# Gate and up projections with features on the partitions: 128-column weight pieces stationary, 256 tokens moving

## The chip, the cores and the metric

The kernel runs on one core of a Trainium2 chip. The metric is the device time of one execution in microseconds (us); three runs of the kernel before gave 2680.31, 2683.87 and 2687.0 us.

## What is computed

Two transformer-like blocks in float32 over one sequence of 256 tokens of width 2048. The change touches two places. The first is the gated feed-forward part that closes block one (hidden width 5632), the second is the Fourier mixer of block two (hidden width 4096, groups of 256 features):

```python
h2 = _modulate(_rms(x, norm2_w[i]), shift2, scale2).astype(x.dtype)
ffn = (jax.nn.silu(h2 @ w_ffn_gate[i]) * (h2 @ w_ffn_up[i])) @ w_ffn_down[i]
...
def fourier_mixer(h, w_in, w_out):
    b, l, _ = h.shape
    u, gate = jnp.split(h @ w_in, 2, axis=-1)
    ug = u.reshape(b, l, C_GROUPS, C_GROUP_DIM).astype(jnp.float32)
    f = jnp.fft.fft2(ug, axes=(1, 3), norm="ortho").real.astype(h.dtype)
    y = f.reshape(b, l, C_WIDTH) * jax.nn.silu(gate)
    return y @ w_out
```

Both have one form: a gate projection, an up projection, a product of silu(gate) with the up result (in the Fourier mixer with its two-dimensional transform), and a down projection. Everything before, between and after them (state space mixer, attention, norms, modulation) is left as it is.

## The kernel before

**Precision.** A float32 product is made of three matmuls on numbers that are split in a high and a low part (`float32r`): high by high, high by low, low by high. Activations stand turned, with the 2048 inputs on the partitions: `hh` and `hl` are [128, 16, 256] (16 k-tiles, 256 tokens). Weights are streamed from memory in units of 256 rows by 512 columns (512 KB): the SyncE queue loads a unit in one of 8 raw slots (`load`, L179), ScalarE writes its high part (`high`, L185), VectorE its low part (`low`, L191), TensorE uses it (`multiply`, L198). There are 4 slots for the split units: ScalarE may write unit u only when TensorE has finished unit u - 4 (semaphore `s_mm`).

**A unit on TensorE (`multiply`).** For each of 2 k-tiles and 2 token tiles it issues three matmuls (L206, L207, L208): a 128 x 128 piece of `hh` or `hl` is stationary and 512 weight columns move. That is 12 matmuls with 512 columns. The result has tokens on the partitions: PSUM banks 0 and 1 take the gate, banks 2 and 3 the up result.

**The steps.** Class `Hidden` (L1418) describes either part. A step c handles 512 hidden features and its order is written out by hand for each engine: units j = 0 to 7 are the gate, 8 to 15 the up projection, 16 to 23 are the down projection of the step before (the first step has 16 units, and 8 down units stand behind the last). The feed-forward part has 11 steps, the Fourier mixer 8, so the gate and up projections are 16 x 19 = 304 units. TensorE walks through them in `hidden_pe` (L1761), ScalarE in `hidden_act` (L1512), VectorE in `hidden_dve` (L1596), SyncE in `hidden_sp` (L1436).

**Between up and down.** ScalarE makes silu of the gate at its j = 11 (L1496). In the feed-forward part VectorE multiplies it with the up result at its j = 19 (L1564) into `hid` [128 tokens, 2, 512]. In the Fourier mixer VectorE copies the up result to `ub` (L1559), TensorE does the first transform after unit 19 (`hidden_dft1_pe`), ScalarE stores it at its j = 23 (`hidden_store_act`), TensorE does the second after unit 3 of the next step (`hidden_dft2_pe`), and VectorE combines and multiplies at its j = 7 (`hidden_product_dve`, L1566).

**The turn.** The down projection needs the hidden features on the partitions, so TensorE turns `hid` in two groups of four 128 x 128 transposes into PSUM bank 6 (`hidden_turn_pe`, L1700, the transposes are L1713). ScalarE makes the high part `hidh` from that bank (L1483), VectorE the low part `hidl` (L1489). The second group waits until VectorE has read the first (semaphore `H.l`). `TURN_AT` gives the places: in the feed-forward part TensorE turns after units 1 and 9 and the other two work at their j = 6 and 14; in the Fourier mixer after units 9 and 12, and at 13 and 16. At the end of each part (`hidden_end_pe`, and for the feed-forward part the head of the context stage, L1973) the turn of the last step stands right ahead of its down units.

**Down projection.** `hidden_down_pe` (L1746) has `hidh` and `hidl` stationary and 512 weight columns moving, and the change leaves that as it is.

**Other work on TensorE in these steps** are modulation rounds (L266) and sums (L354), one or two in a step. A piece of code elsewhere, `ctx_mult` (L1909), already multiplies the other way round: 128 weight columns stationary, 256 tokens of `ch_h` and `ch_l` moving (L1924, L1925, L1926).

## Time and profile before

| | before |
|---|---|
| median of 3 runs | 2683.87 us (2680.31 to 2687.0) |
| profiled execution | 2680.69 us |
| its span, first to last instruction | 2678.9 us |
| TensorE matmul busy | 2496.6 us, 93% |
| TensorE weight loads busy | 1935.3 us, 72% |
| VectorE busy | 1637.4 us, 61% |
| ScalarE busy | 1035.1 us, 39% |
| memory traffic, mean over the span | 220 GB/s |
| feed-forward steps | about 603 to 1404 us of the span |
| Fourier mixer steps | about 2027 to 2679 us of the span |

A busy TensorE says that matmuls are in flight, not how fast they follow each other: a matmul with 512 columns is recorded with about 0.39 us, and the next one begins 0.23 us after its start. What a matmul takes from the engine is the distance between starts, so these are read from the order of instructions in time. The profiled execution lasted 1.8 us longer than its span.

### The profile page before, as it was taken

Reading aid. Unit: us, or ns where it says so; the run is one execution under the profiler, and the core shown is the slowest. Engines: PE = TensorE matmul, PEld = TensorE weight load, DVE = VectorE, ACT = ScalarE, POOL = GpSimd, SP = SyncE. Lnnn points to the kernel's source line nnn. Section 1 sums busy time; section 2 is a strip of 40 time slices with the busy share of each in tenths; the row PEclk is TensorE's granted clock in tenths of the full one; section 3 lists DMA queues with packets and bytes.
Section 4 is the critical chain, followed back from the end, with each engine's and each line's share of the span. In section 5 each row is a group of like instructions: output and inputs, shape, how many; then the busy total and the mean of one; then the engine's idle time right before and its main releaser. Section 6 shows DMA issues by size and latency. Waiting matters only on the chain.

```text
span 2678.9 us, 30714 instructions
## 1 busy us (share of the span) xinstructions
PE 2496.6 (93%) x11822; PEld 1935.3 (72%) x11822; DVE 1637.4 (61%) x1954; ACT 1035.1 (39%) x1370; POOL 214.9 (8%) x193
## 2 busy tenths in 40 slices
PE   5899787989999999999999999999897999999995
PEld 1588665558777777777777887777675788888884
DVE  8544544356777887775667565443466485765556
ACT  2343654224333333333343454444332333334331
POOL 0127810002000000000011000000002000000000
PEclk8799898999999999999999999998897999999997
DMA  9744458986999999997453753333364476675451
GB/s 392 271 150 134 125 216 302 342 334 223 344 338 350 360 338 333 338 336 271 152 173 108 236 154 112 97 97 118 113 194 141 162 249 193 217 239 178 154 171 40
DMA packets 278034, 588.99 MB, mean 220 GB/s; under 512 B 20608, under 2 KB 29824, under 8 KB 276608
## 3 DMA queue, kind: packets, MB, share of 16 engines
q1 hardware_dynamic: 277888, 587.02, 63.6%
q8 instruction: 94, 1.54, 0.2%
q14 instruction: 52, 0.43, 0.0%
HBM read 584.85 MB, written 2.10 MB: 219 GB/s over the span
## 4 chain that ended last, share of the span: by engine, by line
PE 84%; DVE 5%; DMA 3%; POOL 3%; ACT 2%; issue 2%; SPq 0%; DVEq 0%; ACTq 0%; POOLq 0%
PE psum L206 24%; PE psum L208 23%; PE psum L207 23%; PE psum L266 3%; DMA start_slots<-in_w_ada 2%; PE psum L2340 1%; POOL pool_scan_tmp L765 1%; PE psum L1725 1%; DVE wlo L195 1%; PE psum L2315 1%; PE psum L2314 1%; POOL xacc L765 1%; PE psum L1713 1%; DMA x<-in_x 1%; PE psum L681 1%
## 5 line engine op out<-in xcount | busy, mean ns | idle before, releaser
L195 DVE TENSOR_TENSOR wlo<-raw,whi 128x1024 fp32r<-128x1024 f32 (+2 forms) x728 | 880.1, 1227 | 685.1 <-ACT whi L189 672.3
L189 ACT CAST whi<-raw 128x1024 fp32r<-128x1024 f32 (+2 forms) x728 | 738.2, 1025 | 976.2 <-PE psum L208 886.0
L206 PE MATMUL psum<-whi,hh 128*128 128x512 f32 (+1 forms) x2080 | 844.2, 406 | 35.4 <-DVE wlo L195 34.8
L208 PE MATMUL psum<-whi,hl 128*128 128x512 f32 (+1 forms) x2080 | 819.4, 394 | 0.0
L207 PE MATMUL psum<-wlo,hh 128*128 128x512 f32 (+1 forms) x2080 | 817.3, 393 | 0.0
L206 PEld LDWEIGHTS psum<-whi,hh 128*128 128x128 f32 x2080 | 395.9, 190 | 160.7 <-issue 66.8
L208 PEld LDWEIGHTS psum<-whi,hl 128*128 128x128 f32 x2080 | 395.4, 190 | 89.1
L207 PEld LDWEIGHTS psum<-wlo,hh 128*128 128x128 f32 x2080 | 396.5, 191 | 82.7 <-issue 2.9
L206 PE MATMUL psum<-whi,hidh 128*128 128x512 f32 x608 | 247.6, 407 | 8.0 <-DVE wlo L195 6.0
L207 PE MATMUL psum<-wlo,hidh 128*128 128x512 f32 x608 | 243.3, 400 | 0.0
L208 PE MATMUL psum<-whi,hidl 128*128 128x512 f32 x608 | 243.0, 400 | 0.0
L343 DVE SCALAR_TENSOR_TENSOR powers<-araw,cond,powers 128x512 f32<-128x512 f32 x300 | 225.2, 751 | 14.4 <-DVE powers L343 0.5
L402 POOL TENSOR_TENSOR rstd<-ms,mhalf 128x2 f32<-128x2 f32 x7 | 9.9, 1409 | 2027.8 <-DVE ms L387 744.4
L206 PEld LDWEIGHTS psum<-whi,hidh 128*128 128x128 f32 x608 | 116.1, 191 | 43.9 <-issue 14.0
L208 PEld LDWEIGHTS psum<-whi,hidl 128*128 128x128 f32 x608 | 116.0, 191 | 28.3
L207 PEld LDWEIGHTS psum<-wlo,hidh 128*128 128x128 f32 x608 | 116.2, 191 | 27.8 <-issue 0.7
L1588 DVE TENSOR_TENSOR xacc<-xacc,psum 128x1024 f32<-128x1024 f32 x68 | 82.9, 1219 | 29.9 <-PE psum L208 29.9
L266 PE MATMUL psum<-start_slots,cond_windows 128*32 128x512 f32 x256 | 47.5, 845 | 35.4 <-DMA start_slots<-in_w_ada 35.4
L266 PEld LDWEIGHTS psum<-start_slots,cond_windows 128*32 128x32 f32 x256 | 7.5, 133 | 69.0 <-issue 68.9
L414 PE MATMUL psum<-ident,xacc 128*128 128x128 f32 x128 | 25.2, 343 | 33.5 <-DVE xacc L396 21.3
L439 POOL TENSOR_TENSOR hl<-h,hh 128x512 fp32r<-128x512 f32 x32 | 46.6, 1465 | 118.6 <-ACT hh L434 118.6
L414 PEld LDWEIGHTS psum<-ident,xacc 128*128 128x128 f32 x128 | 19.4, 176 | 39.7 <-DVE xacc L396 21.7
(345 smaller groups left out, 2091.5 us busy)
## 6 DMA issues: line engine op xcount, KB each, us to landing
araw<-in_ada_w SPq DMA_DIRECT2D x128, 512.0 KB, 6.5
raw<-in_w_in_fourier SPq DMA_DIRECT2D x128, 512.0 KB, 4.1
raw<-in_w_ffn_gate SPq DMA_DIRECT2D x88, 512.0 KB, 9.6
raw<-in_w_ffn_up SPq DMA_DIRECT2D x88, 512.0 KB, 7.6
raw<-in_w_ffn_down SPq DMA_DIRECT2D x88, 512.0 KB, 9.7
raw<-in_w_in_attn SPq DMA_DIRECT2D x88, 512.0 KB, 4.3
araw<-in_w_ada SPq DMA_DIRECT2D x80, 512.0 KB, 6.2
start_slots<-in_w_ada SPq DMA_DIRECT2D x64, 512.0 KB, 7.7
```

The lines of the kernel that those rows point to most:

```text
L189: nc.scalar.copy(whi[:, u % SPLITS, 0:kn, 0:w], raw[:, u % RING, 0:kn, 0:w]).then_inc(s_hi, 1)
L195: nc.vector.tensor_tensor(wlo[:, u % SPLITS, 0:kn, 0:w], raw[:, u % RING, 0:kn, 0:w], whi[:, u % SPLITS, 0:kn, 0:w].bitcast(F32), ALU.subt ...
L206: nc.tensor.matmul(o, ah[:, kt + k, a], h, start=(kt + k == first_kt), stop=False)
L207: nc.tensor.matmul(o, ah[:, kt + k, a], lw, start=False, stop=False)
L208: ins = nc.tensor.matmul(o, al[:, kt + k, a], h, start=False, stop=(kt + k == last_kt))
L266: ins = nc.tensor.matmul(psum[32 * g:32 * g + 32, SET_BANKS[st][0]], condz[:, vectors - 1, kt, 3 - pi:35 - pi], slot(2 * r + e)[0][:, half ...
L343: ins = nc.vector.scalar_tensor_tensor(out=dst, in0=w, scalar=s, in1=dst, op0=ALU.mult, op1=ALU.add)
L414: ins = nc.tensor.transpose(psum[:, banks[r % 2], j * S + t * P:j * S + t * P + P], xn[:, t, kt * P:(kt + 1) * P], ident[:])
L439: nc.gpsimd.tensor_tensor(ol[:, 2 * r:2 * r + 2], h32[:, r % 2], oh[:, 2 * r:2 * r + 2].bitcast(F32), ALU.subtract).then_inc(s_hl, 1)
L681: ins = nc.tensor.matmul(psum[:, 4 + b, 32 * g:32 * g + 32], W[:, ri, 16 * b + g].rearrange("p i c -> p (i c)"), cpad[:, ri, 16 * b + g], ...
L765: ch(isa.tensor_tensor(o, a, b, op))
L1588: nc.vector.tensor_tensor(o, o, psum[:, BANK[n]:BANK[n] + 2], ALU.add).then_inc(H.dv, 1)
```

## The change

Gate and up units are multiplied by a new function, `multiply_turned`. For each of 2 k-tiles and 4 pieces of 128 weight columns it issues three matmuls with the weight piece stationary and the 256 tokens of `hh` or `hl` moving: 24 matmuls with 256 columns. The result has 128 features on the partitions and 256 tokens on the free axis, two pieces in each PSUM bank; banks, silu and product keep their shapes, and `hid` is already what the down projection wants. `hidden_turn_pe` and its semaphore `H.t` go. ScalarE and VectorE split `hid` directly from SBUF, at j = 6 and 9 (feed-forward) or 11 and 13 (Fourier). The two transforms keep the number and the shapes of their matmuls and work on the turned arrangement: the first now sums over features, the second over tokens. The down projection waits for the low part of each half at its first and second unit.

```diff
@@ -206,6 +206,18 @@
                 nc.tensor.matmul(o, ah[:, kt + k, a], h, start=(kt + k == first_kt), stop=False)
                 nc.tensor.matmul(o, ah[:, kt + k, a], lw, start=False, stop=False)
                 ins = nc.tensor.matmul(o, al[:, kt + k, a], h, start=False, stop=(kt + k == last_kt))
+        ins.then_inc(s_mm, 1)
+
+    def multiply_turned(pe, u, kt, bank):
+
+        pe.wait_ge(s_lo, u + 1)
+        for k in range(2):
+            for f in range(4):
+                o = psum[:, bank + f // 2, f % 2 * S:(f % 2 + 1) * S]
+                h, lw = (w[:, u % SPLITS, k, f * P:(f + 1) * P] for w in (whi, wlo))
+                nc.tensor.matmul(o, h, hh[:, kt + k], start=(kt + k == 0 and f % 2 == 0), stop=False)
+                nc.tensor.matmul(o, lw, hh[:, kt + k], start=False, stop=False)
+                ins = nc.tensor.matmul(o, h, hl[:, kt + k], start=False, stop=(kt + k == KT - 1 and f % 2 == 1))
         ins.then_inc(s_mm, 1)
 
     def lat(b0):
@@ -1419,8 +1431,8 @@
         def __init__(self, name, u0, wg, wu, wd, gcol, ucol, steps, fourier):
             self.u0, self.wg, self.wu, self.wd, self.gcol, self.ucol = u0, wg, wu, wd, gcol, ucol
             self.steps, self.fourier = steps, fourier
-            self.sg, self.a, self.t, self.h, self.l, self.dv, self.ub, self.f1, self.v, self.f2 = (
-                sem(name + n) for n in ("_silu", "_product", "_turned", "_high", "_low", "_added", "_up", "_dft1",
+            self.sg, self.a, self.h, self.l, self.dv, self.ub, self.f1, self.v, self.f2 = (
+                sem(name + n) for n in ("_silu", "_product", "_high", "_low", "_added", "_up", "_dft1",
                                         "_dft1_stored", "_dft2"))
 
         def unit(self, c, j):
@@ -1475,18 +1487,18 @@
             src = w_rows(H.wd, 4 * (c - 1) + 2 * (jj % 2), 2)[:, :, (jj // 2) * CW:(jj // 2 + 1) * CW]
             load(sp, H.u0 + 24 * c - 8 + jj, src)
 
-    def hidden_turn_act(act, H, c, r):
-
-        act.wait_ge(H.t, c * 2 + (r - 1))
+    def hidden_high_act(act, H, c, r):
+
+        act.wait_ge(H.a, c)
         if r == 0:
             act.wait_ge(s_mm, H.used(c, -1))
-        nc.scalar.copy(hidh[:, 2 * r:2 * r + 2], psum[:, 6].rearrange("p (a b) -> p a b", a=2)).then_inc(H.h, 1)
-
-    def hidden_turn_dve(dve, H, c, r):
+        nc.scalar.copy(hidh[:, 2 * r:2 * r + 2], hid4[:, 2 * r:2 * r + 2]).then_inc(H.h, 1)
+
+    def hidden_low_dve(dve, H, c, r):
         dve.wait_ge(H.h, c * 2 + (r - 1))
         if r == 0:
             dve.wait_ge(s_mm, H.used(c, -1))
-        nc.vector.tensor_tensor(hidl[:, 2 * r:2 * r + 2], psum[:, 6].rearrange("p (a b) -> p a b", a=2),
+        nc.vector.tensor_tensor(hidl[:, 2 * r:2 * r + 2], hid4[:, 2 * r:2 * r + 2],
                                 hidh[:, 2 * r:2 * r + 2].bitcast(F32), ALU.subtract).then_inc(H.l, 1)
 
     def hidden_silu_act(act, H, c):
@@ -1500,14 +1512,15 @@
         act.wait_ge(H.f1, c + 1)
         if c >= 1:
             act.wait_ge(H.f2, c)
-        o = dfts[:].rearrange("p (g h) k -> p h g k", g=2)
-        v = psum[:, 2:4].rearrange("p h (g k) -> p h g k", g=2)
+        o = dfts[:].rearrange("p (g t) k -> p t g k", g=2)
+        v = psum[:, 2:4].rearrange("p t (g k) -> p t g k", g=2)
         nc.scalar.copy(o[:, :, :, 0:129], v[:, :, :, 0:129])
         nc.scalar.copy(o[:, :, :, 257:384], v[:, :, :, 129:256])
         nc.scalar.copy(o[:, :, :, 129:256], v[:, :, :, 127:0:-1])
         nc.scalar.mul(o[:, :, :, 385:512], v[:, :, :, 255:128:-1], -1.0).then_inc(H.v, 1)
 
-    TURN_AT = {False: ((1, 6), (9, 14)), True: ((9, 13), (12, 16))}
+    PARTS_AT = {False: (6, 9), True: (11, 13)}
+    hid4 = hid[:].rearrange("p t (f s) -> p (t f) s", f=2)
 
     def hidden_act(act, H, c):
         first = isinstance(c, int) and c == 0
@@ -1517,8 +1530,8 @@
         for j in range(4 if first else 0, 16 if first else 24):
             if not first:
                 for r in range(2):
-                    if j == TURN_AT[H.fourier][r][1]:
-                        hidden_turn_act(act, H, c, r)
+                    if j == PARTS_AT[H.fourier][r]:
+                        hidden_high_act(act, H, c, r)
             if j == 11:
                 hidden_silu_act(act, H, c)
             if not H.fourier and c == 9:
@@ -1544,7 +1557,7 @@
     def hidden_end_act(act, H):
         c = H.steps
         for r in range(2):
-            hidden_turn_act(act, H, c, r)
+            hidden_high_act(act, H, c, r)
         for jj in range(8):
             high(act, H.u0 + 24 * c - 8 + jj)
 
@@ -1560,7 +1573,8 @@
         else:
             dve.wait_ge(H.sg, c + 1)
             if later:
-                dve.wait_ge(H.t, c * 2)
+                dve.wait_ge(H.h, c * 2)
+                dve.wait_ge(H.l, c * 2)
             nc.vector.tensor_tensor(hid[:], sgb[:], psum[:, 2:4], ALU.mult).then_inc(H.a, 1)
 
     def hidden_product_dve(dve, H, c):
@@ -1568,10 +1582,11 @@
         dve.wait_ge(H.f2, c + 1)
         dve.wait_ge(H.sg, c + 1)
         if not isinstance(c, int) or c >= 1:
-            dve.wait_ge(H.t, c * 2)
-        o = ub[:].rearrange("p t (g k) -> p t g k", g=2)
-        v = psum[:, 2:4].rearrange("p t (g k) -> p t g k", g=2)
-        even, odd = v[:, :, :, 1:128], hid[:].rearrange("p t (g k) -> p t g k", g=2)[:, :, :, 129:256]
+            dve.wait_ge(H.h, c * 2)
+            dve.wait_ge(H.l, c * 2)
+        o = ub[:].rearrange("p g (h k) -> p g h k", h=2)
+        v = psum[:, 2:4].rearrange("p g (h k) -> p g h k", h=2)
+        even, odd = v[:, :, :, 1:128], hid[:].rearrange("p g (h k) -> p g h k", h=2)[:, :, :, 129:256]
         ch = chd[0]
         ch(nc.vector.tensor_copy(odd, v[:, :, :, 129:256]))
         ch.wait()
@@ -1604,8 +1619,8 @@
         for j in range(4 if first else 0, n):
             if not first:
                 for r in range(2):
-                    if j == TURN_AT[H.fourier][r][1]:
-                        hidden_turn_dve(dve, H, c, r)
+                    if j == PARTS_AT[H.fourier][r]:
+                        hidden_low_dve(dve, H, c, r)
                 if second and j == 3 and not H.fourier:
                     hidden_up_dve(dve, H, 0)
                 if not second and j in (1, 3):
@@ -1654,7 +1669,7 @@
             hidden_add_dve(dve, H, c - 1, n)
         hidden_product_dve(dve, H, c - 1)
         for r in range(2):
-            hidden_turn_dve(dve, H, c, r)
+            hidden_low_dve(dve, H, c, r)
         for jj in range(8):
             low(dve, H.u0 + 24 * c - 8 + jj)
             if jj in (5, 7):
@@ -1697,34 +1712,17 @@
                 nc.vector.scalar_tensor_tensor(out=x[:, t, cs], in0=x[:, t, cs], scalar=rstd[:, t], in1=lnb[:, cs],
                                                op0=ALU.mult, op1=ALU.add).then_inc(s_post, 1)
 
-    def hidden_turn_pe(pe, H, c, r):
-
-        if r == 0:
-            pe.wait_ge(H.a, c * 1)
-            if c >= 2:
-                pe.wait_ge(s_mod, (16 + 2 * (c > 2) + 2 * (c > 4)) if H.fourier else min(2 * c - 2, 16))
-            if not isinstance(c, int) or c >= 2:
-                pe.wait_ge(H.l, c * 2 - 2)
-        else:
-            pe.wait_ge(H.l, c * 2 - 1)
-        for j in range(2):
-            for t in range(TT):
-                k = 2 * r + j
-                ins = nc.tensor.transpose(psum[:, 6, j * S + t * P:j * S + t * P + P], hid[:, t, k * P:(k + 1) * P],
-                                          ident[:])
-        ins.then_inc(H.t, 1)
-
     def hidden_dft1_pe(pe, H, c):
 
         pe.wait_ge(H.ub, c + 1)
         if c == 0:
             pe.wait_ge(s_dft, 48)
-        for half in range(2):
+        for t in range(TT):
             for g in range(2):
-                for t in range(TT):
-                    ins = nc.tensor.matmul(psum[:, 2 + half, g * S:(g + 1) * S],
-                                           ub[:, t, g * S + half * P:g * S + half * P + P], dft[:, t],
-                                           start=(t == 0), stop=(t == TT - 1))
+                for half in range(2):
+                    ins = nc.tensor.matmul(psum[:, 2 + t, g * S:(g + 1) * S],
+                                           ub[:, g, half * S + t * P:half * S + t * P + P], dft[:, half],
+                                           start=(half == 0), stop=(half == 1))
         ins.then_inc(H.f1, 1)
 
     def hidden_dft2_pe(pe, H, c):
@@ -1733,21 +1731,22 @@
         if c == 0:
             pe.wait_ge(s_zero, 3)
         for g in range(2):
-            for t in range(TT):
-                o = psum[:, 2 + t, g * S:(g + 1) * S]
-                for half in range(2):
-                    nc.tensor.matmul(o[:, 0:129], dfts[:, 2 * g + half, t * P:t * P + P], dft[:, half, 0:129],
-                                     start=(half == 0), stop=(half == 1))
-                for half in range(2):
-                    ins = nc.tensor.matmul(o[:, 129:256], dfts[:, 2 * g + half, S + t * P:S + t * P + P], dft2[:, half, 1:128],
-                                           start=(half == 0), stop=(half == 1))
+            for half in range(2):
+                o = psum[:, 2 + g, half * S:(half + 1) * S]
+                for t in range(TT):
+                    nc.tensor.matmul(o[:, 0:129], dfts[:, 2 * g + t, half * P:half * P + P], dft[:, t, 0:129],
+                                     start=(t == 0), stop=(t == TT - 1))
+                for t in range(TT):
+                    ins = nc.tensor.matmul(o[:, 129:256], dfts[:, 2 * g + t, S + half * P:S + half * P + P], dft2[:, t, 1:128],
+                                           start=(t == 0), stop=(t == TT - 1))
         ins.then_inc(H.f2, 1)
 
     def hidden_down_pe(pe, H, c, jj, unit):
 
         n = jj // 2
+        if jj < 2:
+            pe.wait_ge(H.l, c * 2 - 1 + jj)
         if jj == 0:
-            pe.wait_ge(H.l, c * 2)
             if isinstance(c, int) and c == H.steps:
                 pe.wait_ge(H.dv, 4 * c - 5)
             else:
@@ -1774,15 +1773,12 @@
             if j == 8 and not first:
                 pe.wait_ge(H.a, c * 1)
             if j < 16:
-                multiply(pe, tiles=lat(2 * (j // 8)), kt=2 * (j % 8), last_kt=KT - 1, **H.unit(c, j))
+                multiply_turned(pe, H.unit(c, j)["u"], 2 * (j % 8), 2 * (j // 8))
                 if first and j < 4:
                     turn_pe(pe, k, xn, kn, j + 4, j + 5)
             else:
                 hidden_down_pe(pe, H, c, j - 16, H.unit(c, j))
             if not first:
-                for r in range(2):
-                    if j == TURN_AT[H.fourier][r][0]:
-                        hidden_turn_pe(pe, H, c, r)
                 if H.fourier and j == 3:
                     hidden_dft2_pe(pe, H, c - 1)
                 if H.fourier and j == 19:
@@ -1810,8 +1806,6 @@
         c = H.steps
         if H.fourier:
             hidden_dft2_pe(pe, H, c - 1)
-        for r in range(2):
-            hidden_turn_pe(pe, H, c, r)
         for jj in range(8):
             hidden_down_pe(pe, H, c, jj, {"u": H.u0 + 24 * c - 8 + jj})
 
@@ -1972,7 +1966,7 @@
         for n in (2, 3):
             hidden_add_dve(dve, ffn, c - 1, n)
         for r in range(2):
-            hidden_turn_dve(dve, ffn, c, r)
+            hidden_low_dve(dve, ffn, c, r)
         for k in range(-8, 3 * UPC):
             if k == -8:
                 dve.wait_ge(s_growc, 8)
```

## Rows read from the trace of the kernel before

**Rows 1.** The page of the profile: busy time of each engine.
```profile
PE 2496.6 (93%) x11822; PEld 1935.3 (72%) x11822; DVE 1637.4 (61%) x1954; ACT 1035.1 (39%) x1370; POOL 214.9 (8%) x193
```

**Rows 2.** By window: busy PE, PEld, DVE, ACT, POOL; granted clock, DMA share, GB/s.
```profile
764.00:838.00 74.00, 74.00 (x352) 57.03 (x344) 58.06 (x65) 27.21 (x28) 0.00 (x0) 1.00 0.93 341
...
2252.00:2326.00 74.00, 74.00 (x344) 61.24 (x343) 45.56 (x46) 28.63 (x32) 0.00 (x0) 1.00 0.59 196
```

**Rows 3.** TensorE in time (start, length in us): gate and up units, 34 starts apart.
```profile
2283.17 0.39 PE L208 MATMUL psum<-whi,hl 128*128 128x512 f32 x1
...
2290.95 0.39 PE L206 MATMUL psum<-whi,hidh 128*128 128x512 f32 x1
```

**Rows 4.** TensorE in time: 256 tokens moving over stationary weights, 28 starts apart.
```profile
1483.81 0.28 PE L1925 MATMUL psum<-ctxh,wlo 128*128 128x256 f32 x1
...
1487.16 0.28 PE L1926 MATMUL psum<-ctxl,whi 128*128 128x256 f32 x1
```

**Rows 5.** TensorE in time: the same stage with 512 weight columns moving, 24 starts apart.
```profile
1446.28 0.39 PE L206 MATMUL psum<-whi,ctxh 128*128 128x512 f32 x1
...
1451.91 0.39 PE L206 MATMUL psum<-whi,ctxh 128*128 128x512 f32 x1
```

**Rows 6.** TensorE in time: stationary activations, 320 weight columns moving, 95 starts apart.
```profile
1509.90 0.31 PE L206 MATMUL psum<-whi,hh 128*128 128x320 f32 x1
...
1523.83 0.31 PE L208 MATMUL psum<-whi,hl 128*128 128x320 f32 x1
```

**Rows 7.** TensorE in time: sixteen matmuls with one column each.
```profile
861.95 1.84 PE L354 MATMUL psum<-ones,powers 128*128 128x1 f32 x16
863.65 0.48 PE L206 MATMUL psum<-whi,hidh 128*128 128x512 f32 x1
```

**Rows 8.** Groups of weight loads by shape (busy us, mean ns).
```profile
L1924 PEld LDWEIGHTS psum<-ctxh,whi 128*128 128x128 f32 x16 | 3.0, 188 | 1.4 <-DVE wlo L195 1.4
```

**Rows 9.** The line of the transposes: count, lengths, first and last start.
```profile
L1713 PE MATMUL psum<-ident,hid x152: 270/272/476, 659.9 to 2629.9; 128*128 128x128 f32 x152
```

**Rows 10.** TensorE in time around one group of transposes.
```profile
807.50 0.39 PE L208 MATMUL psum<-whi,hl 128*128 128x512 f32 x1
807.74 0.60 PE L1713 MATMUL psum<-ident,hid 128*128 128x128 f32 x4
...
808.41 0.40 PE L207 MATMUL psum<-wlo,hh 128*128 128x512 f32 x1
```

**Rows 11.** All engines in time: the end of the feed-forward part.
```profile
1392.98 0.40 PE L208 MATMUL psum<-whi,hidl 128*128 128x512 f32 x1
...
1393.42 1.22 DVE L1588 TENSOR_TENSOR xacc<-xacc,psum 128x1024 f32<-128x1024 f32 x1 [4.40 <-PE psum L208]
1393.86 0.59 ACT L1483 CAST hidh<-psum 128x512 fp32r<-128x512 f32 x1 [10.57 <-PE psum L1713]
...
1397.61 3.50 DVE L195 TENSOR_TENSOR wlo<-raw,whi 128x1024 fp32r<-128x1024 f32 x3 [0.31 <-ACT whi L189]
1398.98 0.77 PE L206 MATMUL psum<-whi,hidh 128*128 128x512 f32 x1 [3.03 <-DVE wlo L195]
```

**Rows 12.** All engines in time: the end of the Fourier mixer.
```profile
2625.50 1.23 DVE L1582 TENSOR_TENSOR hid<-sgb,ub 128x1024 f32<-128x1024 f32 x1
...
2631.91 4.63 DVE L195 TENSOR_TENSOR wlo<-raw,whi 128x1024 fp32r<-128x1024 f32 x4 [0.26 <-ACT whi L189]
2633.28 0.77 PE L206 MATMUL psum<-whi,hidh 128*128 128x512 f32 x1 [2.97 <-DVE wlo L195]
```

**Rows 13.** Who waited for whom, 640 to 1400 us (total us, times, longest).
```profile
ACT whi L189 <- PE psum L208: 400.4, 213, 4.2
...
PE psum L206 <- DVE wlo L195: 3.0, 1, 3.0
```

**Rows 14.** In time: VectorE's low parts of units 8 and 9, TensorE starting unit 9.
```profile
819.27 2.47 DVE L195 TENSOR_TENSOR wlo<-raw,whi 128x1024 fp32r<-128x1024 f32 x2
...
828.63 0.39 PE L206 MATMUL psum<-whi,hh 128*128 128x512 f32 x1
```

## Prediction

> **What bounds the kernel now.** I read the page first: TensorE is busy for 93% of the span, no other engine for more than 61% [rows 1]. A share says little by itself, so the second view is busy time by window. In a feed-forward step and in a Fourier step TensorE is busy for the whole window at a granted clock of 1.00, its upper level of 2.4 GHz, while VectorE is busy for 58.1 of 74.0 us at most and ScalarE for 28.6 [rows 2]. In these steps whatever TensorE does more or less in its instruction stream is on the path that sets the end, to the nanosecond. The third view is TensorE's order in time, because the recorded length of a matmul (0.39 us with 512 columns) overlaps the next one; what counts is the distance between starts. Over 34 starts in gate and up units this is (2290.95 - 2283.17) / 34 = 0.2288 us; I take 0.229 [rows 3].
>
> **Part 1: two matmuls of 256 columns in place of one of 512.** A unit has 12 matmuls now and 24 afterwards; columns that move are the same in number (12 x 512 = 24 x 256). There are 304 such units, so 304 x 12 = 3648 times one distance of 0.229 us is replaced by two distances at 256 columns. The trace has nearly this operation: in the context stage pieces of `whi` and `wlo` are stationary and 256 tokens move. Over 28 starts, four unit borders among them, the distance is (1487.16 - 1483.81) / 28 = 0.1196 us [rows 4]. This is more than half of 0.229. But the same stage with the same activation tile and 512 moving columns is slower too: (1451.91 - 1446.28) / 24 = 0.2346 us [rows 5]. So part of the 0.1196 may belong to that tile and not to the column count. A second way to the number stays with `hh`: with 320 columns its distance is (1523.83 - 1509.90) / 95 = 0.1466 us [rows 6]; the line through 320 and 512 columns has a slope of (0.229 - 0.1466) / 192 = 0.429 ns a column and gives 0.1466 - 64 x 0.000429 = 0.1191 us at 256. In the changed unit the weights are stationary as in rows 4 and `hh` moves, which neither row has. I take 0.1194, between the two and nearer to the row with the same roles: 2 x 0.1194 - 0.229 = 0.0098 us, and 3648 x 0.0098 = +35.8 us. The ends: 0.1196 gives +37.2 us. For the lower end I take the ratio of the two 512-column distances as if it held at 256 as well, 0.1196 x 0.229 / 0.2346 = 0.1167, which gives 3648 x 0.0044 = +16.1 us.
>
> Is there a floor under these small matmuls? Sixteen matmuls with a single column take 863.65 - 861.95 = 1.70 us, 0.106 us each, and about 0.11 with the late first one behind them [rows 7]. So one stationary load with its matmul has room in 0.12 us, with little to spare. Each load is recorded with 188 ns [rows 8]; if loads did not overlap, a unit would take 24 x 0.188 = 4.5 us and the change would cost 500 us, but rows 4 show one every 0.1196 us.
>
> The Trainium skill ("TensorE: Matmul & The Clock Gate", section "Back-to-back issue gap") lists 262 cycles for 256 columns and 518 for 512 at the upper clock. By these figures two matmuls of 256 would cost 2.5 ns more than one of 512, and the part would come to 3648 x 0.0025 = +9 us. The trace disagrees on both sizes: 0.1196 us where the page's cycles are 0.109, 0.229 where they are 0.216. I use the rows.
>
> **Part 2: the transposes go.** There are 152, in 38 groups of four [rows 9]. From the last matmul ahead of a group to the second behind it are 808.41 - 807.50 = 0.91 us [rows 10]; without the group these are two distances, 0.458 us. A group costs 0.45 us (the recorded 0.60 us is length, not cost). 34 groups stand inside a full stream: 34 x 0.45 = -15.3 us.
>
> The other four are at the two ends, where TensorE waits. Feed-forward end: its last matmul starts at 1392.98 and the next down unit at 1398.98 [rows 11]. Without the turn ScalarE can begin when that matmul is done, at about 1393.4 in place of 1393.86, and makes both high halves in a row (0.59 us each), until 1394.5; the first high part of weights follows, until about 1395.5. VectorE has its addition from 1393.42 for 1.22 us, then two low halves, until 1395.9, and the low weights begin there in place of 1397.61. That is 1.7 us earlier, and TensorE with it. Fourier end: the product is ready at 2625.50 + 1.23 = 2626.73 [rows 12]. Two high halves take until 2627.9, high weights until 2628.8, and low weights begin at about 2628.9 in place of 2631.91: 3.0 us. Both ends: -4.7 us.
>
> **Part 3: what is moved.** The splitting of `hid` reads SBUF in place of PSUM, with the same number of elements; it is on ScalarE and VectorE. New waits: ScalarE waits for the product `H.a` at its j = 6 or 11, with the high parts of weights (and in the Fourier mixer silu) queued behind. The product was made on VectorE at j = 19 of the step before or at j = 7, long before. Product and low part wait for each other on VectorE in order, at no cost. TensorE waits for the low halves at j = 16 and 17, made at 6 to 13. The cover is how far the weights' parts run ahead: in 760 us ScalarE waited 213 times for TensorE to free a slot, and TensorE waited for VectorE once, at the end of the part [rows 13]. VectorE had the low part of unit 9 at 821.7, TensorE began this unit at 828.63, 6.9 us later [rows 14]. Moving 0.68 us of VectorE from j = 14 to 9 is nothing against that, and every unit gives VectorE 0.12 us more. If the cover were gone, 38 halves of 0.6 us would cost 23 us. The transforms have the same counts and shapes: 0. SyncE's queue is not touched, and memory at 341 GB/s with a share of 0.93 in rows 2 only gets more time.
>
> **The sum.** +35.8 - 15.3 - 4.7 = +15.8 us. Against the profiled execution of 2680.69 us that is 2696.5. This execution lies 3.2 us under the median 2683.87 of the three runs shown, so I state 2699.7 us, +0.6%.
>
> **The rivals.**
> A, the forecast: small matmuls cost as above. Chance 0.66.
> B, the cost stays with the tile: if the distance at 256 columns comes out at 0.1167, the change costs 16.1 - 20.0 = -4 us, 2680 us, no difference. It turns at (0.229 + 20.0 / 3648) / 2 = 0.1172 us: below that the change does not lose. For it speaks that `hh` as an operand gives 2.4% shorter distances than the context tile at 512 columns; against it that the line by `hh` itself gives 0.1191. Chance 0.18.
> C, time goes by columns alone, with nothing for each matmul: 2 x 0.1145 = 0.229, part 1 is 0, and only the gains stay: 2664 us. For it: nothing but the floor of rows 7, which lies under 0.1145. Against it: rows 4. The skill's figures in part 1 belong here, at +9 - 20 = -11 us. Chance 0.08.
> D, borders: with starts so close to the floor TensorE's sequencer has no lead, and each unit's wait on the low part shows. Priced by a quarter of a matmul distance at 512, 0.06 us, in 304 units: 18 us more, 2718 us. Against it: four borders in rows 4 cost nothing. Chance 0.08.
>
> **How the numbers follow.** About 0.3% (8 us) is what a measurement of this kernel can tell from no change. In A the change stays within it if the distance is below 0.1183 us, which I give 0.04 of A's 0.66. So slower has 0.62 + 0.08 = 0.70, same 0.04 + 0.18 = 0.22, faster 0.08. The range takes in B and its few us of spread between runs, 2677, and above A's upper end, 0.1196 (2701), half of D and the spread between runs: 2712. C and most of D are left out.
>
> **What the profile after would show.** Starts in gate and up units at 0.1194 us (2.87 us a unit, 2.75 now); no transposes; a step of the feed-forward part longer by 16 x 12 x 0.0098 - 0.9 = 1.0 us; the waits for low weights at the two ends shorter by 1.7 and 3.0 us; clock 1.00 inside the steps. Wrong would make it: a distance under 0.1172; TensorE waiting for VectorE or ScalarE inside a step; a unit's first start late; a clock below 1.00.

## The result, and the profile after

The changed kernel takes 2666.6 us (median of 5 runs, 2665.8 to 2669.8); the kernel before, timed beside it, 2680.3 (5 runs, 2678.1 to 2687.0). The ratio is 0.9945, with an interval of 0.993 to 0.996: 13.7 us faster, where 16 us slower was forecast, with a range of 2677 to 2712 us. The profiled execution took 2667.0 us, its span is 2665.2 (2678.9 before).

First the page of the profile after (busy time by engine), then two windows of 74 us, in the feed-forward part and in the Fourier mixer, in the columns of [rows 2].

```profile
PE 2481.1 (93%) x15318; PEld 2083.2 (78%) x15318; DVE 1637.1 (61%) x1954; ACT 1034.3 (39%) x1370; POOL 214.3 (8%) x193
```

```profile
764.00:838.00 74.00, 74.00 (x542) 65.45 (x542) 59.25 (x67) 27.20 (x27) 0.00 (x0) 1.00 0.96 347
2252.00:2326.00 74.00, 74.00 (x525) 69.19 (x524) 47.66 (x50) 28.67 (x31) 0.00 (x0) 1.00 0.64 216
```

Matmuls went from 11822 to 15318: 3648 more, less 152 transposes, as the change says. TensorE still fills the windows at a clock of 1.00, so what it is given there is still the path. The answer to [rows 3], the order of TensorE in time, has two faces. Two stretches of gate and up units, 48 starts each:

```profile
1027.08 0.28 PE L220 MATMUL psum<-hl,whi 128*128 128x256 f32 x1
...
1032.52 0.28 PE L220 MATMUL psum<-hl,whi 128*128 128x256 f32 x1
...
1100.02 0.28 PE L220 MATMUL psum<-hl,whi 128*128 128x256 f32 x1
...
1105.67 0.28 PE L220 MATMUL psum<-hl,whi 128*128 128x256 f32 x1
```

The first stretch has (1032.52 - 1027.08) / 48 = 0.1133 us a start, the second, one step later and with the same instructions, (1105.67 - 1100.02) / 48 = 0.1177. All long stretches of the trace lie at one of these two values, or within 0.0004 us of them, and none changes inside: what breaks a stretch (down units, other small matmuls) is where the level can change. Taken from the first start of a unit to its last, 116 of the 304 units are at the low level, and 188 at the high one or slowed at the head of a stretch. The mean inside the stretches, where the clock is 1.00, is 0.1157 us. Neither level is near the 0.1194 of the forecast.

A step of the feed-forward part shows it by the sum. The first gate matmul of three steps in a row:

```profile
1017.88 0.39 PE L218 MATMUL psum<-hh,whi 128*128 128x256 f32 x1
...
1090.49 0.39 PE L218 MATMUL psum<-hh,whi 128*128 128x256 f32 x1
...
1164.75 0.39 PE L218 MATMUL psum<-hh,whi 128*128 128x256 f32 x1
```

The low step lasts 72.61 us, the high one 74.26; before, a step lasted 73.9. By the terms of the forecast a step should change by 384 x 0.1133 - 192 x 0.229 - 0.9 = -1.4 or by 384 x 0.1177 - 192 x 0.229 - 0.9 = +0.3 us, and it does.

The end of the feed-forward part, all engines in time (the answer to [rows 11]):

```profile
1385.10 0.40 PE L208 MATMUL psum<-whi,hidl 128*128 128x512 f32 x1
1385.53 1.22 DVE L1603 TENSOR_TENSOR xacc<-xacc,psum 128x1024 f32<-128x1024 f32 x1 [4.41 <-PE psum L208]
1385.59 1.14 ACT L1495 CAST hidh<-hid 128x512 fp32r<-128x512 f32 x2 [10.20 <-PE psum L208]
1386.63 3.89 ACT L189 CAST whi<-raw 128x1024 fp32r<-128x1024 f32 x4
1386.67 1.28 DVE L1501 TENSOR_TENSOR hidl<-hid,hidh 128x512 fp32r<-128x512 f32 x2
1387.88 2.35 DVE L195 TENSOR_TENSOR wlo<-raw,whi 128x1024 fp32r<-128x1024 f32 x2
...
1389.24 0.76 PE L206 MATMUL psum<-whi,hidh 128*128 128x512 f32 x1 [3.75 <-DVE wlo L195]
```

The gap from 1385.10 to 1389.24 is 4.1 us, before it was 6.0 [rows 11]. And the end of the Fourier mixer (the answer to [rows 12]):

```profile
2611.38 0.61 PE L1740 MATMUL psum<-dft,dfts 128*128 128x127 f32 x4
...
2614.14 1.23 DVE L1597 TENSOR_TENSOR hid<-sgb,ub 128x1024 f32<-128x1024 f32 x1
2615.40 1.14 ACT L1495 CAST hidh<-hid 128x512 fp32r<-128x512 f32 x2 [15.20 <-DVE hid L1597]
...
2617.52 2.36 DVE L195 TENSOR_TENSOR wlo<-raw,whi 128x1024 fp32r<-128x1024 f32 x2 [0.17 <-ACT whi L189]
2618.89 0.77 PE L206 MATMUL psum<-whi,hidh 128*128 128x512 f32 x1 [6.90 <-DVE wlo L195]
```

From VectorE's start on the last product to the next down unit: 4.75 us, before 2633.28 - 2625.50 = 7.78 [rows 12], so 3.0 us less. Both ends gave what they were forecast to give.

### The profile page after: what moved, and what is told of

Read it like the earlier page. It is cut to its first block, busy times and chain, and to the rows that moved or that the text cites. A ratio compares the mean times of both kernels' runs of the same rounds, so it can differ in the third digit from the quotient of the medians.

```text
span 2665.2 us, 37725 instructions
## 1 busy us (share of the span) xinstructions
PE 2481.1 (93%) x15318; PEld 2083.2 (78%) x15318; DVE 1637.1 (61%) x1954; ACT 1034.3 (39%) x1370; POOL 214.3 (8%) x193
## 4 chain that ended last, share of the span: by engine, by line
PE 84%; DVE 5%; DMA 3%; POOL 3%; ACT 2%; issue 2%; SPq 0%; DVEq 0%; ACTq 0%; POOLq 0%
PE psum L206 13%; PE psum L208 13%; PE psum L207 13%; PE psum L218 11%; PE psum L219 11%; PE psum L220 11%; PE psum L278 3%; DMA start_slots<-in_w_ada 2%; PE psum L2334 1%; POOL pool_scan_tmp L777 1%; PE psum L1723 1%; DVE wlo L195 1%; PE psum L2309 1%; PE psum L693 1%; PE psum L2308 1%
## 5 line engine op out<-in xcount | busy, mean ns | idle before, releaser
L218 PE MATMUL psum<-hh,whi 128*128 128x256 f32 x2432 | 686.6, 282 | 4.4 <-DVE wlo L195 4.4
L219 PE MATMUL psum<-hh,wlo 128*128 128x256 f32 x2432 | 679.8, 280 | 0.0
L220 PE MATMUL psum<-hl,whi 128*128 128x256 f32 x2432 | 679.7, 279 | 0.0
L218 PEld LDWEIGHTS psum<-hh,whi 128*128 128x128 f32 x2432 | 460.0, 189 | 26.8 <-issue 25.9
L220 PEld LDWEIGHTS psum<-hl,whi 128*128 128x128 f32 x2432 | 463.0, 190 | 0.0
L219 PEld LDWEIGHTS psum<-hh,wlo 128*128 128x128 f32 x2432 | 459.2, 189 | 1.3 <-issue 1.0
L206 PE MATMUL psum<-whi,hh 128*128 128x512 f32 (+1 forms) x864 | 354.8, 411 | 29.4 <-DVE wlo L195 28.9
L208 PE MATMUL psum<-whi,hl 128*128 128x512 f32 (+1 forms) x864 | 340.8, 394 | 0.0
L207 PE MATMUL psum<-wlo,hh 128*128 128x512 f32 (+1 forms) x864 | 339.5, 393 | 0.0
L207 PEld LDWEIGHTS psum<-wlo,hh 128*128 128x128 f32 x864 | 166.2, 192 | 34.3 <-issue 1.9
## 6 DMA issues: line engine op xcount, KB each, us to landing
raw<-in_w_ffn_gate SPq DMA_DIRECT2D x88, 512.0 KB, 10.8
```

Source lines behind the costliest of these rows:

```text
L206: nc.tensor.matmul(o, ah[:, kt + k, a], h, start=(kt + k == first_kt), stop=False)
L207: nc.tensor.matmul(o, ah[:, kt + k, a], lw, start=False, stop=False)
L208: ins = nc.tensor.matmul(o, al[:, kt + k, a], h, start=False, stop=(kt + k == last_kt))
L218: nc.tensor.matmul(o, h, hh[:, kt + k], start=(kt + k == 0 and f % 2 == 0), stop=False)
L219: nc.tensor.matmul(o, lw, hh[:, kt + k], start=False, stop=False)
L220: ins = nc.tensor.matmul(o, h, hl[:, kt + k], start=False, stop=(kt + k == KT - 1 and f % 2 == 1))
```

## The experiments

All are the changed kernel with one edit (in one case two), unless it is said that they are the kernel before. "Units low" counts the gate and up units at 0.1133 us, out of 304; the changed kernel has 116. Each ratio is to the kernel before, timed beside the run. The first question: is the level of the 256-column distance chance, or the roles of the operands, or the order of accumulation? The second, when none of these fitted: is it where the tiles lie in SBUF?

**The changed kernel again**, unaltered.

> The changed kernel, unaltered, profiled a second time. Its first profile shows two steady distances between starts in gate and up units: 0.1133 us (first step and steps 1 to 6 of the feed-forward part, first step of the Fourier mixer) and 0.1177 us (from step 7 on, and the other Fourier steps). If the level is fixed by the place in the instruction stream, the same units show the same level again and the time is within 2 us of 2666.6. If it is a state that the engine falls into, the units at 0.1133 and 0.1177 are others this time; each unit moved from one level to the other moves the time by 24 x 0.0044 = 0.11 us, so anything between 2650 (all low) and 2682 (all high).

2665.7 us (2663.7 to 2670.9), ratio 0.995 [0.9933, 0.9967]. 114 units are low. They are the same ones but for six units, three in the last feed-forward step and three at the start of the second Fourier step. So the levels are, but for a few units, not drawn anew in each execution.

**The kernel before, its gate and up matmuls in halves.** The activations stay stationary and the transposes stay; only the 512 columns are cut in two.

```diff
+                for half in range(2):
+                    c = slice(half * S, (half + 1) * S)
+                    o = psum[:, bank + t, c]
+                    h, lw = whi[:, u % SPLITS, k, c], wlo[:, u % SPLITS, k, c]
...
-                multiply(pe, tiles=lat(2 * (j // 8)), kt=2 * (j % 8), last_kt=KT - 1, **H.unit(c, j))
+                multiply_halves(pe, H.unit(c, j)["u"], 2 * (j % 8), 2 * (j // 8))
```

> The kernel before (activations stationary, the turn kept) with one edit: in gate and up units each matmul of 512 weight columns is made as two of 256. It changes the size alone, not the roles. Theory 1 (a matmul costs by its columns, whatever is stationary): distances of 0.113 to 0.118 us, the time changes by 3648 x (2 x 0.1155 - 0.229) = +7 us, between -9 and +24. Theory 2 (with stationary activations the line through 320 and 512 columns holds, and the gain came from the exchange of roles): 0.1191 us, +34 us.

2704.0 us, ratio 1.0096 [1.0063, 1.0128]. TensorE in time:

```profile
1042.42 0.28 PE L220 MATMUL psum<-whi,hh 128*128 128x256 f32 x1
...
1048.07 0.28 PE L220 MATMUL psum<-whi,hh 128*128 128x256 f32 x1
...
1192.69 0.28 PE L220 MATMUL psum<-whi,hh 128*128 128x256 f32 x1
...
1198.13 0.28 PE L220 MATMUL psum<-whi,hh 128*128 128x256 f32 x1
```

5.65 / 48 = 0.1177 and 5.44 / 48 = 0.1133: the same two values with the roles exchanged. Nearly all stretches here are at the high one, and 3648 x (2 x 0.1177 - 0.229) = +23 us is what the run shows over the kernel before. So which operand is stationary does not set the two values, though it or the rest of the kernel changes their mix (14 units low); and part 1 alone does cost time, as the forecast said, at a smaller size: +23 us where +35.8 was forecast.

**The changed kernel without its part 1**: gate and up by 512 columns again, with no turn of the product behind them (the product is used unturned, so the numbers it computes are others).

```diff
-                multiply_turned(pe, H.unit(c, j)["u"], 2 * (j % 8), 2 * (j // 8))
+                multiply(pe, tiles=lat(2 * (j // 8)), kt=2 * (j % 8), last_kt=KT - 1, **H.unit(c, j))
```

> The changed kernel with the old multiplication in gate and up units (stationary activations, 512 columns), and still no turn: only the transposes are gone. What is computed is not the reference's, since the product is used unturned. By the prediction's part 2 this is the kernel before minus 34 x 0.45 - 4.7 = 20.0 us, 2660 us. If the transposes had been cheaper than thought or something takes their place, less than 15 us. Against the changed kernel at 2666.6 it should be 6 us faster, if small matmuls cost 0.1158 us on average.

2657.0 us, ratio 0.9921 [0.9895, 0.9946]: 21 us less than the kernel before by the ratio (14 to 28), 24 between the medians. Steps of the Fourier mixer went from 76.17 and 74.37 us, in turn, to 75.27 and 73.48, 0.90 less each, which is two groups of transposes at 0.45. Part 2 stands with its -20.0 us. The run also measures part 1 in place, since it differs from the changed kernel in nothing else: 2666.6 - 2657.0 = +9.6 us. In the two traces the time from the start of each gate or up matmul to the next start on TensorE, one wait left out of each, adds up to 847.2 and 856.8 us: +9.6 again.

**Six matmuls in a row into one PSUM place**: the loop over the four pieces outside, the one over k inside.

```diff
-        for k in range(2):
-            for f in range(4):
+        for f in range(4):
+            for k in range(2):
```

> The changed kernel with the two loops of a unit exchanged: the piece outside, the k-tile inside, so that 6 matmuls in a row (in place of 3) accumulate in the same 256 columns of PSUM, as nearer to the context stage, where the distance is 0.1196 us and all 48 matmuls go to one place. If accumulating in one place costs distance, it rises from 0.113 to 0.118 to about 0.1196: +7296 x 0.0038 = +28 us. If what matters there is the moving tile, no change: 2664 to 2669 us.

2666.0 us, ratio 0.9947 [0.9931, 0.9962], with the same 116 units low. The order of accumulation does nothing.

**32 bytes left empty** ahead of the tiles of the mixers. In the compiled program `whi` and `wlo` begin at a multiple of 128 bytes in each partition and so do the pieces of them that a matmul reads; `hh` and `hl` begin 64 bytes past one, `hidh`, `hidl` and the context tile 96 past one. (These places follow from the order and the sizes of the tiles in the kernel.) The edit takes these last three to a multiple of 128.

```diff
+    pad_hidden = sb(ctx, "pad_hidden", [P, 8])
     m = ExitStack()
```

> The changed kernel with 32 bytes a partition of unused padding ahead of the tiles of the later stages. `hh` and `hl` stay where they are; `hidh`, `hidl`, the context tiles and the others behind them move from addresses that are 32 over a multiple of 64 to multiples of 64. Theory 1 (an operand that begins off a multiple of 64 bytes costs TensorE distance): down units, whose matmuls with 512 columns stand 0.2342 us apart, come to the 0.229 us of the units with `hh`, 608 x 3 = 1824 matmuls x 0.0053 = -9.7 us; the context stage's 256 columns come from 0.1196 to 0.113 to 0.118; the time is about 2656. Gate and up units keep their two levels. Theory 2 (the tile's distance has another cause): no distance changes, 2664 to 2669.

2661.3 us, ratio 0.9939 [0.9917, 0.9962]. The down units, which had (1014.68 - 1006.25) / 36 = 0.2342 us a start in the changed kernel, here have 0.2325:

```profile
1006.90 0.40 PE L207 MATMUL psum<-whi,hidh 128*128 128x512 f32 x1
...
1015.27 0.40 PE L207 MATMUL psum<-whi,hidh 128*128 128x512 f32 x1
```

Neither theory holds: the distance changed, but not to 0.229, and the context stage's 256 columns read 0.1184 to 0.1190 us, not 0.113 to 0.118. Of the gate and up units, whose own tiles did not move, 148 are low in place of 116. The time is less, but the interval overlaps that of the changed kernel; what the run gave is the idea.

**`hh` and `hl` moved by 192 bytes**, to a multiple of 128, with the tiles behind them at one too.

```diff
+    pad_hh = sb(ctx, "pad_hh", [P, 48])
     hh = sb(ctx, "hh", [P, KT, S], F32R)
...
+    pad_hidden = sb(ctx, "pad_hidden", [P, 24])
```

> As e5_pad32, and `hh` and `hl` too are moved, by 192 bytes, so that all matmul operands that are activations begin at multiples of 256 bytes. If finer alignment of the moving tile makes the two levels (0.1133 and 0.1177 us) in gate and up units, all of them come to the lower, 171 units x 24 x 0.0044 = -18 us against e5_pad32. If the levels are not a matter of address, the same units as before show 0.1177 us and the time is that of e5_pad32.

2692.3 us, ratio 1.0058 [1.0033, 1.0082]. TensorE in time: in the attention part 512 columns over `hh`, then a gate stretch of the Fourier mixer:

```profile
1502.21 0.39 PE L208 MATMUL psum<-whi,hh 128*128 128x512 f32 x1
...
1513.36 0.39 PE L208 MATMUL psum<-whi,hh 128*128 128x512 f32 x1
...
2204.41 0.29 PE L220 MATMUL psum<-hh,whi 128*128 128x256 f32 x1
...
2210.17 0.29 PE L220 MATMUL psum<-hh,whi 128*128 128x256 f32 x1
```

11.15 / 48 = 0.2323 where it was 0.229; 5.76 / 48 = 0.1200, and 0.1187 in other stretches. No stretch is left at 0.1133 or 0.1177, so the expectation that alignment brings all of them to the lower level is refuted. By the mean inside its stretches (0.1190) part 1 grows by 7296 x (0.1190 - 0.1157) = 24 us, and the median is 26 over the changed kernel, 31 over the run with 32 bytes left empty, from which it differs only in the place of `hh` and `hl` modulo 128 bytes. (The profiled execution, 2706.0, was the slowest of the seven; its steps are 20.7 us longer in sum.) 192 empty bytes ahead of `hh` cost 1% of the kernel.

**An extra, already met wait on TensorE** ahead of the second feed-forward step, to shift what follows in its instruction stream.

```diff
+        if not H.fourier and c == 1:
+            for _ in range(3):
+                pe.wait_ge(s_one, 16)
```

> The changed kernel with one more instruction in TensorE's stream, a wait that has long been met, ahead of step 1 of the feed-forward part. If the level belongs to a position in the instruction stream, it moves: some units of steps 1 to 6 at 0.1177 us, or some of the later ones at 0.1133. If it belongs to what goes on in the step (other engines, transfers), the pattern of the changed kernel stays: low in steps 1 to 6, high from 7 on.

2666.2 us, ratio 0.9953 [0.9936, 0.997]; the same 116 units are low. (One instruction came of the three.) A shift of the instruction stream by one instruction does not move the levels; larger ones were not tried.

**128 tokens a matmul**, twice as many of them again.

> The changed kernel with each matmul of gate and up units cut again, 128 tokens in place of 256, twice as many. If a load of the stationary operand takes about 0.106 us of the engine (sixteen matmuls with one column took 1.70 us), the distance stays near 0.107 us and a unit takes 48 x 0.107 = 5.1 us: +304 x 2.4 = +730 us, and 256 columns lie just above the floor. If there is no such floor, the distance halves to 0.057 us and the time stays within 20 us.

3758.7 us, one run. Two stretches of gate units:

```profile
700.10 0.41 PE L220 MATMUL psum<-hh,whi 128*128 128x128 f32 x1
...
705.22 0.41 PE L220 MATMUL psum<-hh,whi 128*128 128x128 f32 x1
...
1002.09 0.28 PE L220 MATMUL psum<-hh,whi 128*128 128x128 f32 x1
...
1007.45 0.28 PE L220 MATMUL psum<-hh,whi 128*128 128x128 f32 x1
```

The later one has 5.36 / 48 = 0.1117 us: with half the columns the distance hardly falls, from 0.1133. This is a floor, a little above the 0.106 of the one-column matmuls [rows 7]. The earlier one, 5.12 / 24 = 0.2133, lies where the granted clock was 0.50, the level of 1.2 GHz; twice as many matmuls at the floor cost 14592 x 0.1117 - 7296 x 0.1157 = 786 us. The rest of the 1092 us over the changed kernel, 306, is about what such stretches cost: the clock stood at 0.50 from 606 to 954 us, 1811 to 1907 and, but for 7 us, 2664 to 2910, together 683 us of which half, 341, is lost. The windows of 100 us:

```profile
700.00:800.00 100.00, 100.00 (x471) 100.00 (x470) 18.95 (x19) 11.35 (x11) 0.00 (x0) 0.50 0.23 76
...
1000.00:1100.00 100.00, 100.00 (x783) 91.56 (x782) 51.68 (x56) 23.83 (x24) 0.00 (x0) 1.00 0.66 221
```

The clock fell at 606 us, while TensorE waited for 8.0 us ahead of the first step. In the changed kernel it fell in the same wait, at 600 us, and was back at 1.00 at 610. Here it stayed down until 954 us, although TensorE was busy for 341 of the 342 us from 612 on. What kept it down is not shown. The fall at 1811 us came with no wait ahead of it.

**96 bytes left empty** ahead of the mixers' tiles, so that `hidh`, `hidl` and the context lie 64 past a multiple of 128, like `hh`.

```diff
+    pad_hidden = sb(ctx, "pad_hidden", [P, 24])
     m = ExitStack()
```

> The kernel after with 96 bytes a partition left empty ahead of the tiles that hold hidh, hidl and the context: their address goes from 96 to 64 bytes past a multiple of 128, where hh and hl lie. Theory (the address of the activation tile sets the distance of starts): the down units go from 0.234 to 0.229 us a matmul, 1824 x 0.0053 = 9.7 us less, the context's 256-column matmuls from 0.1196 to 0.113-0.118 us; time about 2655 us. Rival (the address of hidh has no effect beyond that of the padding by 32 bytes, or the gain there was chance): the down units stay at 0.2326-0.234 us and the time lies at 2661-2666 us.

2650.7 us (2649.8 to 2652.1), ratio 0.9886 [0.9873, 0.990], the fastest of all. A down stretch and a gate stretch at the place where the changed kernel was at the high level:

```profile
1010.98 0.39 PE L207 MATMUL psum<-whi,hidh 128*128 128x512 f32 x1
...
1019.22 0.39 PE L207 MATMUL psum<-whi,hidh 128*128 128x512 f32 x1
...
1118.03 0.28 PE L220 MATMUL psum<-hh,wlo 128*128 128x256 f32 x1
...
1123.47 0.28 PE L220 MATMUL psum<-hh,wlo 128*128 128x256 f32 x1
```

8.24 / 36 = 0.2289 and 5.44 / 48 = 0.1133. The down units give 1824 x 0.0053 = 9.7 us. Low units are 209 of 304, most of the new ones in the Fourier mixer, and the mean inside the stretches falls from 0.1157 to 0.1141, another 7296 x 0.0016 = 11.7 us. In the feed-forward part some units went to the low level and about as many to the high one; the gain is in the Fourier mixer. The sum, 21, is what the two parts lost in the profiled execution (20.5), and more than the 16 between the medians; the profiled executions differ also by 4.4 us in when the first step begins (608.56 and 612.98), ahead of the units that the edit speeds up.

The context stage, from which the forecast took its 0.1196, is the same code in all these runs. With its tile at 64 bytes from the weights it reads:

```profile
1473.09 0.28 PE L1921 MATMUL psum<-ctxl,whi 128*128 128x256 f32 x1
...
1475.81 0.28 PE L1921 MATMUL psum<-ctxl,whi 128*128 128x256 f32 x1
```

2.72 / 24 = 0.1133 us: the very operation of [rows 4] comes to a level of `hh` when its tile is moved.

**The kernel before with the same 96 bytes.**

> The kernel before with the same 96 bytes left empty. Theory: hidh and the context read as above, down units 0.229 us, 9.7 us less and a few us more in attention: about 2670 us, so that the distance between the two kernels with the padding stays near the 14 us that it has without. Rival (the kernel before gains nothing by it): 2680 us.

2671.7 us, ratio 0.9961 [0.9948, 0.9975]. Its down stretch:

```profile
1014.82 0.39 PE L207 MATMUL psum<-whi,hidh 128*128 128x512 f32 x1
...
1023.06 0.39 PE L207 MATMUL psum<-whi,hidh 128*128 128x512 f32 x1
```

And its context stage, the place of [rows 4]:

```profile
1482.23 0.28 PE L1927 MATMUL psum<-ctxl,whi 128*128 128x256 f32 x1
...
1485.41 0.28 PE L1927 MATMUL psum<-ctxl,whi 128*128 128x256 f32 x1
```

8.24 / 36 = 0.2289 again, and 3.18 / 27 = 0.1178, the other level of `hh`. The 8.4 us between the medians fit the 9.7 of the down units. With the padding in both, the change is worth 2671.7 - 2650.7 = 21 us in place of 14, since most of its gate and up units (209 of 304) are at 0.1133, where two of them cost 0.2266 and one of 512 costs 0.229.

**64 bytes left empty ahead of `whi`**: everything that a matmul reads moves by the same 64 bytes.

```diff
+    pad_w = sb(ctx, "pad_w", [P, 16])
     whi = sb(ctx, "whi", [P, SPLITS, 2, CW], F32R)
```

> The kernel after with 64 bytes left empty ahead of whi: whi, wlo, hh, hl, hidh and all later tiles move together by 64 bytes, so the distances between the addresses stay as they are, while hh is now at a multiple of 128. Theory that the distance between the two operands' addresses counts: nothing changes, gate and up 0.1133 and 0.1177 us, 2666 us. Rival, that the moving or stationary activation's own address counts: gate and up 0.1187-0.120 us as where hh alone was moved there, about 2690 us, and hidh (32 past a multiple of 128) at a distance not seen yet.

2667.4 us, ratio 0.9948 [0.9934, 0.9961]. The gate stretches are at 0.1133 and 0.1177 in the same places (the same 116 units low), the down units at 0.2342. The two stretches that answer those of the changed kernel:

```profile
1030.03 0.28 PE L221 MATMUL psum<-hl,whi 128*128 128x256 f32 x1
...
1035.47 0.28 PE L221 MATMUL psum<-hl,whi 128*128 128x256 f32 x1
...
1102.08 0.28 PE L221 MATMUL psum<-hl,whi 128*128 128x256 f32 x1
...
1107.73 0.28 PE L221 MATMUL psum<-hl,whi 128*128 128x256 f32 x1
```

`hh` is here at a multiple of 128, where it cost 0.119 to 0.120 above, and costs nothing. So it is not the address of a tile by itself that counts but its distance from tiles that moved with it. The weights are the ones among these that the same matmul reads, which is why the distance is taken here from the other operand; a third tile was not moved by itself to rule it out.

**32 bytes left empty ahead of `hh`**: `hh` 96 bytes past a multiple of 128, as the context tile is in the kernel before.

```diff
+    pad_hh = sb(ctx, "pad_hh", [P, 8])
     hh = sb(ctx, "hh", [P, KT, S], F32R)
```

> The kernel after with 32 bytes left empty ahead of hh: hh and hl lie 96 bytes past a multiple of 128, where the context tile lies in the kernel before, whose 256-column matmuls started 0.1196 us apart; later tiles lie at a multiple of 128. Theory (the 0.1196 us of the context belongs to its tile's address): gate and up 0.1196 us throughout, 3648 x 2 x (0.1196 - 0.1158) = 28 us over the kernel after, less about 3 us in the down units: about 2691 us. Rival (the 0.1196 us belongs to something else of the context's matmuls, its sources or its stage): 0.113-0.118 us, about 2663 us.

2697.4 us (2681.6 to 2700.3, 10 runs), ratio 1.0044 [1.0026, 1.0063]; the profiled execution, 2683.1, was among its fastest. A gate stretch, and 512 columns over `hh`:

```profile
1110.09 0.28 PE L219 MATMUL psum<-hh,whi 128*128 128x256 f32 x1
...
1115.77 0.28 PE L219 MATMUL psum<-hh,whi 128*128 128x256 f32 x1
...
1530.69 0.40 PE L207 MATMUL psum<-whi,hh 128*128 128x512 f32 x1
...
1541.89 0.40 PE L207 MATMUL psum<-whi,hh 128*128 128x512 f32 x1
```

5.68 / 48 = 0.1183 in every stretch, at one level, and 11.20 / 48 = 0.2333. This is not quite the 0.1196 of [rows 4], but it has left both values that `hh` had. By this distance the gate and up units cost 7296 x (0.1183 - 0.1157) = 19 us more than in the changed kernel, and the down units, now at 0.2325, 3 us less. The sum of 16 us is what the profiled execution shows (2683.1 against 2667.0); the median is 31 over. The spread of 19 us between runs is unexplained.

The distances, by how far the activation tile lies from the weights, modulo 128 bytes:

```text
bytes apart   256 columns                      512 columns
64            0.1133 or 0.1177 (hh)            0.229  (hh; hidh with 96 bytes left empty)
              0.1133, 0.1178 (context, with 96 bytes left empty)
0             0.1187 or 0.1200 (hh)            0.2323 (hh), 0.2325 (hidh)
              0.1184 to 0.1190 (context)
96            0.1183 (hh), 0.1196 (context)    0.2333 (hh), 0.2342 (hidh)
```

32 bytes apart was not tried.

## Why the prediction was wrong

**What bounds the kernel**: right. TensorE fills the steps at a clock of 1.00 before and after, and each step's length changed by what its distances say.

**Part 1** failed, and its failing step is the choice of 0.1194. The distance was taken from [rows 4], because there the weights are stationary as in the changed kernel. The halves in the kernel before showed that the roles do not make the difference: with the activations stationary the distances are 0.1133 and 0.1177 too. What rows 4 had of its own was the place of its tile, 96 bytes from the weights where `hh` is at 64: with that tile at 64, the same code reads 0.1133 in the changed kernel and 0.1178 in the kernel before. The prediction saw a sign of it, [rows 5] against [rows 3], 0.2346 against 0.229 at 512 columns with everything else alike, and put that in the lower end only, as a ratio. A difference between two rows with the same operation and the same shape is a second variable that has not been named; it should have been worked into the likeliest value. The measured mean of 0.1157 lies even under that lower end, 0.1167. The term is +9.6 us, by the changed kernel with and without part 1, where +35.8 was forecast; 3648 x (2 x 0.1157 - 0.229) gives +8.8.

The second way to the number, the line through 320 and 512 columns, stayed with `hh` and still gave 0.1191. Its other point was the fault: the 320-column matmuls start 0.1466 us apart with `hh` at each of the three distances tried. With `hh` 96 bytes from the weights, in the last of the experiments, where 256 and 512 columns had both become slower, they read

```profile
1516.36 0.31 PE L207 MATMUL psum<-whi,hh 128*128 128x320 f32 x1
...
1528.82 0.31 PE L208 MATMUL psum<-wlo,hh 128*128 128x320 f32 x1
```

(1528.82 - 1516.36) / 85 = 0.1466 us as in [rows 6]. So what slows the 512-column row does not slow this one, and a line through the two has no meaning at 256. That it met rows 4 was an accident, and two ways that agree were taken for a proof.

**The floor** in [rows 7] was read rightly: 0.1117 us at 128 columns, 0.106 at one. The Trainium skill ("TensorE: Matmul & The Clock Gate", section "LDWEIGHTS (loading the stationary operand)") gives the columns of the stationary piece by 1.2 as a load's time in ns, 107 for 128 columns. The runs agree with it as a floor (0.1117), not as a length of a load (0.188) [rows 8]. Cutting these matmuls from 256 to 128 columns therefore saved 0.0016 us a start at the most and cost a further start for each piece.

**Part 2** right: the run without part 1 gives -21 us (-28 to -14; -24 between the medians) against -20.0, the steps lost 0.90 us each for two groups, and the ends gained 6.0 - 4.1 = 1.9 and 3.0 us against 1.7 and 3.0.

**Part 3** right: nothing. TensorE waits three times inside the two parts (2.0, 1.3 and 4.4 us, for VectorE), and as long at the same places before; these are not of the change. The new waits for the low halves are met before TensorE comes to them.

**The sum** with the measured term: +9.6 - 20.0 = -10.4 us. The medians differ by 13.7 (the ratio's interval is 11 to 19 us). The two profiled executions, 13.7 apart as well, say where the rest is:

| stretch of the span | before | after | |
|---|---|---|---|
| start to the first gate matmul | 607.5 | 608.6 | +1.1 |
| from there to the first down unit after the last step | 791.5 | 780.7 | -10.8 |
| from there to the Fourier mixer | 633.1 | 630.0 | -3.1 |
| Fourier mixer, to the end | 646.8 | 645.9 | -0.9 |

The two parts that the change touches give -11.7. The -3.1 lies between them, where TensorE's code is the same, and stays open.

That the sum came out as a gain also hangs on the mix of the two levels, which nobody chose: with every unit at 0.1177 it would be 3648 x (2 x 0.1177 - 0.229) - 20.0 = +3 us, with every unit at 0.1133 it would be -29.

**The rivals.** D, a cost at the borders, is refuted: the 48 starts of each stretch above contain borders of units, at no cost. B gave the right cause, that the cost stays with the tile, at 2680 us, and C, columns alone, gave the nearest time, 2664 us, for a reason that is not true: two halves cost 0.2354 us at the high level, more than 0.229. Both had too little of the chance. The Trainium skill's figures ("TensorE: Matmul & The Clock Gate", section "Back-to-back issue gap"), 262 cycles for 256 columns and 518 for 512, gave +9 us for the part, and +9.6 was measured. But the distances were not its 0.109 and 0.216, and neither level has its ratio; the mean of the two comes near it by luck.

**What stays open**: what decides between 0.1133 and 0.1177 at the same address. It goes by place in the program, but for a few units. The order of accumulation and a shift by one instruction do not change it; with the roles exchanged both levels are there, but nearly all units are high. It is decided at the head of a stretch and holds to its end; and moving `hidh`, which the gate matmuls do not read, changes it, in the feed-forward part both ways. The units ahead of a gate stretch read `hidh`, so their rhythm may set it. That is argued, not shown. Nor is it shown why an address costs at all.

## What to carry to other kernels

Before a duration is carried from one row to another, compare two rows of the same operation and shape on the two tiles: if they differ (here 0.2346 and 0.229), the tile is a part of the price. In a kernel bound by a long stream of matmuls a few percent of the stream can lie in where the two operands stand to each other in SBUF: it is worth trying 32, 64 and 96 empty bytes ahead of a tile, since 96 ahead of the mixers' tiles gave 16 us in the changed kernel, more than the change itself, for one line, and 8 in the kernel before. And a padding tried for one stage must be read in all stages, since it moves every tile behind it: 192 bytes ahead of `hh`, with 96 more ahead of the mixers' tiles, cost 26 us.

## What the hardware showed that was not expected

- In these runs the distance between starts goes with the distance between the two operands' addresses modulo 128 bytes: at 512 columns 0.229 us at 64 bytes, 0.2323 and 0.2325 at 0, 0.2333 and 0.2342 at 96; and moving both operands by 64 bytes leaves it. At 320 columns it is 0.1466 us at all three. The Trainium skill ("SBUF — State Buffer", section "Who interferes with whom") gives TensorE two independent read ports, one for the moving operand and one for loads. Read as saying that the two operands cannot disturb each other, it does not fit these runs; it says nothing of addresses.
- At 256 columns and 64 bytes apart there are two steady distances, 0.1133 and 0.1177 us, at a granted clock of 1.00 in both, that repeat by place from one execution to the next (116 and 114 of 304 units low, all but six units alike).
- 128 columns start 0.1117 us apart, 256 columns 0.1133: a floor, and at a clock of 0.50 it was 0.2133.
- A fall of the granted clock to 0.50 in a wait of 8.0 us lasted 10 us in the changed kernel and 348 us in the run with 128 columns, with TensorE busy again behind the wait in both.
